# Block inverse of the delta net: from the second level on, even and odd heads on the two 64-row halves of the TensorE array

## What is computed

```python
k_beta = k * beta[..., None]
L = jnp.where(strict, jnp.einsum('bhncd,bhnjd->bhncj', k_beta, k) * decay, 0.0)
uw = lax.linalg.triangular_solve(eye + L, rhs, left_side=True, lower=True, unit_diagonal=True)
```

## Time and profile before

| | |
|---|---|
| median of three runs | 1870.41 us |
| span of the profiled execution, first to last instruction | 1869.1 us |
| the median less that span (the profiled execution's own whole time is not given apart) | 1.3 us |
| TensorE matmul busy, share of the span | 96% |
| VectorE, ScalarE | 49%, 32% |
| mean granted TensorE clock | 0.991 |

### The profile page before, as it was taken

The page is one execution under the profiler, slowest core; times in us unless marked ns, Lnnn a source line. Parts: engine busy times, 40 slices in busy tenths (PEclk is TensorE's granted clock), DMA queues, the critical chain, the costliest instruction groups (busy, mean ns, idle before and its releaser), DMA issues.

```text
span 1869.1 us, 23868 instructions
## 1 busy us (share of the span) xinstructions
PE 1789.6 (96%) x9684; PEld 1276.0 (68%) x9684; DVE 924.8 (49%) x1574; ACT 603.1 (32%) x1089; POOL 42.6 (2%) x61
## 2 busy tenths in 40 slices
PE   7999999999988999999999999999989999999996
PEld 7878888888867787777776767799773333333332
DVE  5354555555575553554447665574663333323234
ACT  6433233323233332233335542573421111111112
POOL 0000000000000000000000000000021000000000
PEclk9999999999999999999999999999999999999999
DMA  7412222222122222212222122210399999999996
GB/s 275 159 68 91 71 99 81 89 79 102 68 102 79 69 88 80 79 68 102 79 79 79 46 91 90 91 46 13 136 354 392 420 421 420 420 421 420 421 420 261
DMA packets 50751, 325.63 MB, mean 174 GB/s; under 512 B 8088, under 2 KB 8264, under 8 KB 14032
## 3 DMA queue, kind: packets, MB, share of 16 engines
q1 hardware_dynamic: 44320, 305.38, 41.7%
q0 software_dynamic: 6032, 17.39, 2.7%
q10 hardware_dynamic: 288, 1.31, 0.2%
HBM read 322.45 MB, written 5.31 MB: 175 GB/s over the span
## 4 chain that ended last, share of the span: by engine, by line
PE 76%; DMA 10%; DVE 7%; ACT 3%; issue 3%; DVEq 0%; ACTq 0%; SPq 0%; POOLq 0%
PE PJ L583 16%; PE PJ L585 15%; PE PJ L584 15%; PE PJ L2596 8%; PE PJ L2610 4%; DMA m_a<-in_w_moe 3%; DMA m_c<-in_w_moe 3%; DMA m_b<-in_w_moe 3%; PE PB L2622 2%; PE PB L2240 2%; PE PB L2201 1%; PE PB L2233 1%; PE PJ L2347 1%; DVE x L1490 1%; DVE w_lo L1288 1%
## 5 line engine op out<-in xcount | busy, mean ns | idle before, releaser
L583 PE MATMUL PJ<-hT_hi,w_hi 128*128 128x512 f32 x832 | 338.8, 407 | 7.5 <-DVE x L1490 6.1
L585 PE MATMUL PJ<-hT_hi,w_lo 128*128 128x512 f32 x832 | 325.4, 391 | 0.0
L1288 DVE TENSOR_TENSOR w_lo<-w_raw,w_hi 128x1024 fp32r<-128x1024 f32 (+1 forms) x224 | 228.2, 1031 | 196.4 <-ACT w_hi L801 195.6
L584 PE MATMUL PJ<-hT_lo,w_hi 128*128 128x512 f32 x832 | 324.7, 390 | 0.0
L801 ACT ACTIVATE w_hi<-w_raw 128x1024 fp32r<-128x1024 f32 (+1 forms) x224 | 196.1, 899 | 26.1 <-PE PJ L585 24.6
L583 PEld LDWEIGHTS PJ<-hT_hi,w_hi 128*128 128x128 f32 x832 | 156.7, 188 | 54.6 <-issue 20.7
L585 PEld LDWEIGHTS PJ<-hT_hi,w_lo 128*128 128x128 f32 x832 | 156.4, 188 | 34.3
L584 PEld LDWEIGHTS PJ<-hT_lo,w_hi 128*128 128x128 f32 x832 | 156.9, 189 | 33.4 <-issue 3.4
L856 ACT ACTIVATE sc<-sc,stats 128x256 f32<-128x256 f32 (+2 forms) x80 | 43.4, 542 | 328.4 <-DVE stats L1371 328.4
L1948 DVE TENSOR_TENSOR x<-x,PB 128x512 f32<-128x512 f32 x128 | 79.4, 681 | 87.6 <-PE PB L2622 87.5
L583 PE MATMUL PJ<-w_hi,hT_hi 128*128 128x256 f32 x384 | 110.3, 287 | 3.0 <-DVE rt L1449 3.0
(11 more groups left out here) (437 smaller groups left out, 2796.7 us busy)
## 6 DMA issues: line engine op xcount, KB each, us to landing
w_raw<-in_w_all SPq DMA_DIRECT2D x92, 1024.0 KB, 4.8
m_b<-in_w_moe SPq DMA_DIRECT2D x86, 1024.0 KB, 26.6
m_a<-in_w_moe SPq DMA_DIRECT2D x66, 1024.0 KB, 26.0
m_c<-in_w_moe SPq DMA_DIRECT2D x20, 1024.0 KB, 27.1
m_d<-in_w_moe SPq DMA_DIRECT2D x10, 1024.0 KB, 27.6
m_e<-in_w_moe SPq DMA_DIRECT2D x10, 1024.0 KB
aux<-scr_c POOLq DMA_DIRECT2D x6, 512.0 KB, 3.9
aux<-in_decay POOLq DMA_DIRECT2D x6, 512.0 KB, 4.1
```

The source lines that it names most:

```text
L583: pe.matmul(dst, lh, rh, start=start, stop=False)
L584: pe.matmul(dst, lh, rl, start=False, stop=False)
L585: return pe.matmul(dst, ll, rh, start=False, stop=stop)
L1288: dve.tensor_tensor(w_lo[:, n % SPLIT, j * w:(j + 1) * w], w_raw[:, n % RAW, j * w:(j + 1) * w], w_hi[:, n % SPLIT, j * w:(j + 1) * w].bit ...
```

## The change

The masks of levels 2 to 6 are written twice, once for each half of the partitions. `u_product` puts heads 0 and 2 on partitions 0 to 63 and heads 1 and 3 on 64 to 127. The mask product then covers 128 rows x 128 columns. `turn` transposes two heads at once (128x128), which puts an even head's rows on 0 to 63 and the odd head's on 64 to 127; it writes columns 256 to 511 of the chunk's bank, and ScalarE copies 128 rows x 256 columns. `level_product` takes rows 0 to 63 for even heads and 64 to 127 for odd ones; even heads of both chunks of a pair go to the first bank of `PJ[c // 2]`, odd heads to the second. So two chunks share two banks, and the waits at these places are for both chunks of the pair (`c | 1`). The last level's transposes are whole ones as before. The diff:

```diff
+        def even_cols(a, l):
+            return a.rearrange("p (a b q two w) -> p a b q two w", a=2, b=2, two=2, w=1 << l)[:, :, :, :, 0, :]
+        def parity_banks(pj, c, l):
+            return pj.rearrange("p (b z a n) -> p b z a n", b=2, z=4, a=2)[:, :, c % 2, :, :].rearrange(
+                "p b a (q w) -> p a b q w", w=1 << l)
...
-                        act.activation(TT[0:rows, c, :], PJ[c // 2][0:rows, (c % 2) * S:(c % 2 + 1) * S],
-                                       ACT.Copy).then_inc(g_T, 1)
+                        bank = PJ[c // 2][:, (c % 2) * S:(c % 2 + 1) * S]
+                        if l < NLVL - 1:
+                            act.activation(TT[:, c, 0:256], bank[:, 256:S], ACT.Copy).then_inc(g_T, 1)
+                        else:
+                            act.activation(TT[:, c, :], bank, ACT.Copy).then_inc(g_T, 1)
...
-                        dve.tensor_tensor(heads64(U[0:rows, c, 0:256]), heads64(PB[c][0:rows, 0:256]), m,
+                        dve.tensor_tensor(heads64(U[:, c, 0:64 * n]), heads64(PB[c][:, 0:64 * n]), m,
                                           ALU.mult).then_inc(g_uc, 1)
...
-                        dve.wait_ge(g_tmm, 4 * (l - 1) + c + 1)
+                        dve.wait_ge(g_tmm, 4 * (l - 1) + (c if l == 1 else c | 1) + 1)
...
+                            dve.tensor_tensor(even_cols(T_[:, c, :], l), even_cols(T_[:, c, :], l),
+                                              parity_banks(PJ[c // 2][:], c, l), ALU.add).then_inc(g_tup, 1)
...
-                            last = pe.matmul(PB[c][0:64, H64[h]], lt_odd(l)[:, c, H64[h]],
+                            last = pe.matmul(PB[c][ROWS[h % 2], H64[h // 2]], lt_odd(l)[:, c, H64[h]],
                                              half(T_[:, c, H4[h]], l, 0), start=True, stop=True)
...
-                    pe.wait_ge(g_T, n + 1)
+                    pe.wait_ge(g_T, n + 1 if l == 1 else 4 * (l - 1) + (c | 1) + 1)
...
+                            o = h % 2 * S + c % 2 * P + h // 2 * 64
+                            last = pe.matmul(PJ[c // 2][:, o:o + 64], TT[ROWS[h % 2], c, H4[h // 2]],
+                                             U[ROWS[h % 2], c, H64[h // 2]], start=True, stop=True)
...
-                    pe.wait_ge(g_tup, 4 * l + c + 1)
                     if l < NLVL - 1:
+                        pe.wait_ge(g_tup, 4 * l + (c if l == 1 else c | 1) + 1)
                         pe.wait_ge(g_col, cols_turn(l, c))
...
-                            last = pe.transpose(pj_(c, h)[0:64, :], U[:, c, 256 + h * 64:256 + (h + 1) * 64], ident)
+                        for i in range(2, 4):
+                            last = pe.transpose(pj_(c, i), U[:, c, H4[i]], ident)
+                    else:
+                        pe.wait_ge(g_tup, 4 * l + (c | 1) + 1)
+                        for h in range(4):
                             last = pe.transpose(pj_(c, h), T_[:, c, H4[h]], ident)
...
-            m = np.concatenate([m.reshape(-1, 2, s, 64)[:, 1].reshape(64, 64), np.zeros((64, 64), bool)])
+            m = np.tile(m.reshape(-1, 2, s, 64)[:, 1].reshape(64, 64), (2, 1))
```

More of the change, by code:

```diff
@@ L1041, in delta_net @@
                                            half(T_[:, c, :], l + 1, 1), ACT.Copy).then_inc(g_col, 1)
-                    rows = 64 if l < NLVL - 1 else P
                     for c in range(4):
                         act.wait_ge(g_tt, 4 * l + c + 1)
-                        act.activation(TT[0:rows, c, :], PJ[c // 2][0:rows, (c % 2) * S:(c % 2 + 1) * S],
-                                       ACT.Copy).then_inc(g_T, 1)
+                        bank = PJ[c // 2][:, (c % 2) * S:(c % 2 + 1) * S]
[3 more added lines that the diff above has]
+                            act.activation(TT[:, c, :], bank, ACT.Copy).then_inc(g_T, 1)
                 def key_sums(c):
@@ L1595, in delta_net @@
                 for l in range(1, NLVL):
-                    rows = P if l == 1 else 64
-                    m = cst[0:rows, C_LVL + l * P:C_LVL + l * P + 64].unsqueeze(1).broadcast_to([rows, 4, 64])
+                    n = 4 if l == 1 else 2
+                    m = cst[:, C_LVL + l * P:C_LVL + l * P + 64].unsqueeze(1).broadcast_to([P, n, 64])
                     for c in range(4):
                         dve.wait_ge(g_umm, 4 * (l - 1) + c + 1)
-                        dve.tensor_tensor(heads64(U[0:rows, c, 0:256]), heads64(PB[c][0:rows, 0:256]), m,
+                        dve.tensor_tensor(heads64(U[:, c, 0:64 * n]), heads64(PB[c][:, 0:64 * n]), m,
                                           ALU.mult).then_inc(g_uc, 1)
@@ L1603, in delta_net @@
                         dve.wait_ge(g_tup, 4 * (l - 1) + c + 1)
-                        dve.wait_ge(g_tmm, 4 * (l - 1) + c + 1)
-                        dve.tensor_tensor(half(T_[:, c, :], l, 0), half(T_[:, c, :], l, 0),
-                                          pj_(c)[:, 0:256].rearrange("p (q w) -> p q w", w=1 << l),
-                                          ALU.add).then_inc(g_tup, 1)
+                        dve.wait_ge(g_tmm, 4 * (l - 1) + (c if l == 1 else c | 1) + 1)
+                        if l == 1:
+                            dve.tensor_tensor(half(T_[:, c, :], l, 0), half(T_[:, c, :], l, 0),
+                                              pj_(c)[:, 0:256].rearrange("p (q w) -> p q w", w=1 << l),
+                                              ALU.add).then_inc(g_tup, 1)
+                        else:
+                            dve.tensor_tensor(even_cols(T_[:, c, :], l), even_cols(T_[:, c, :], l),
+                                              parity_banks(PJ[c // 2][:], c, l), ALU.add).then_inc(g_tup, 1)
                     if 2 <= l < NLVL - 1:
@@ L2323, in delta_net @@
                 H64 = [slice(h * 64, (h + 1) * 64) for h in range(4)]
+                ROWS = H64[0:2]
                 def u_product(l, c):
@@ L2342, in level_product @@
                     n = 4 * (l - 1) + c
-                    rows = P if l == 1 else 64
-                    pe.wait_ge(g_T, n + 1)
+                    pe.wait_ge(g_T, n + 1 if l == 1 else 4 * (l - 1) + (c | 1) + 1)
                     pe.wait_ge(g_uc, n + 1)
                     for h in range(4):
-                        last = pe.matmul(PJ[c // 2][:, (c % 2) * S + h * 64:(c % 2) * S + (h + 1) * 64],
-                                         TT[0:rows, c, H4[h]], U[0:rows, c, H64[h]], start=True, stop=True)
+                        if l == 1:
+                            last = pe.matmul(PJ[c // 2][:, (c % 2) * S + h * 64:(c % 2) * S + (h + 1) * 64],
+                                             TT[:, c, H4[h]], U[:, c, H64[h]], start=True, stop=True)
+                        else:
+                            o = h % 2 * S + c % 2 * P + h // 2 * 64
+                            last = pe.matmul(PJ[c // 2][:, o:o + 64], TT[ROWS[h % 2], c, H4[h // 2]],
+                                             U[ROWS[h % 2], c, H64[h // 2]], start=True, stop=True)
                     last.then_inc(g_tmm, 1)
                 def turn(l, c):
-                    pe.wait_ge(g_tup, 4 * l + c + 1)
                     if l < NLVL - 1:
+                        pe.wait_ge(g_tup, 4 * l + (c if l == 1 else c | 1) + 1)
                         pe.wait_ge(g_col, cols_turn(l, c))
-                    for h in range(4):
-                        if l < NLVL - 1:
-                            last = pe.transpose(pj_(c, h)[0:64, :], U[:, c, 256 + h * 64:256 + (h + 1) * 64], ident)
-                        else:
+                        for i in range(2, 4):
+                            last = pe.transpose(pj_(c, i), U[:, c, H4[i]], ident)
+                    else:
+                        pe.wait_ge(g_tup, 4 * l + (c | 1) + 1)
+                        for h in range(4):
                             last = pe.transpose(pj_(c, h), T_[:, c, H4[h]], ident)
```

## The result

The changed kernel takes 1855.76 us, median of four runs (1853.26 to 1858.03); the kernel before, timed again beside it, 1871.04. The ratio is 0.9913, with 95% between 0.9901 and 0.9925. Predicted were 1854.6, in a range of 1851.5 to 1861.0. The profiled execution has a span of 1853.1 us, 16.0 less than before. One number hides two things that don't belong together: the stretch of the inverse became 17.7 us shorter, more than the 15.8 that were forecast, and the rest of the profiled execution became 1.7 us longer although nothing was changed there.

What follows compares the result with a forecast made beforehand. TensorE alone was taken to bound the inverse, step behind step. Saving 17.4 us at full clock less 1.6 for low clock gives 15.8: span 1869.1 to 1853.3, plus 1.3 is 1854.6 us, range 1851.5 to 1861.

Steps and rivals of the forecast that it cites:

- TensorE's work: Levels 2 to 6: paired u_product 0.93 us instead of 2.01, level_product 1.79 instead of 3.71; turns 0.90 instead of 1.79.
- The change of tiling mode: Turn to u_product: weight columns go from 128 to 64, one more drain per level; without that rule some 0.5 us less.
- The chain: One level, 3 to 5, from level_product to the next: additions, column copy, last turn, u_product; period 4.88 us.
- Level 2 was to take 5.58: Level 2's period, longer because ScalarE does its exponential (1.91 us) and four copies behind level 1's copies.
- The sum at the full clock: Whole inverse, level 1's last turn to L2387: starts at 1269.45 instead of 1287.07 - 0.2, saving 17.4 us.
- The clock: Granted clock in the inverse: today's low stretches vanish, a third of the new one runs low; 17.4 - 1.6 = 15.8 us saved.
- the 4.9 us of slow turns: Three low-clock stretches at levels 2, 4 and 6 of the kernel before; their cost is taken back within the 17.4.
- the third of the new stretch that I put at the low clock: A third of the new inverse at 1.2 GHz, given TensorE's idle gaps of some 0.9 us in 4.88: -1.6 us.
- end of 6.0: Upper end of the clock loss in the new inverse; a level wholly at 1.2 GHz lasts 5.9 us.
- The rival of the low clock throughout: New inverse wholly at the low clock, through idle gaps and half the records: saved 11.4 us, 1859.0; chance 0.11.
- What the stretch loses the whole kernel loses: Behind the inverse nothing is tied to absolute time, so everything, experts included, shifts earlier by the full saving.
- The 1.3 us between span and median: Added to the profiled execution's forecast span of 1853.3 us to give the median forecast of 1854.6.

Runs made afterwards that it cites:

- s_lp: Changed kernel with level_product issuing a chunk pair's four even-head products first, then the four odd-head ones, from level 2 on: 1862.62 us, ratio 0.9942.
- s_all: Changed kernel with the even-head products of all four chunks ahead of the odd-head ones, in u_product and level_product: 1868.98 us, ratio 0.9990.
- s_both: Changed kernel with even-head products of each chunk pair before the odd-head ones, in both level_product and u_product: 1859.82 us, ratio 0.9939.

## Why the prediction came out right

Predicted were 1854.6 us and measured 1855.76. The mechanism is the forecast one; that the number is only 1.2 us off is in part luck, since three terms missed and cancelled (the last three points below).

- **TensorE's work**: right. A pair costs what one cost, for chains of 64-column products too: 0.93 and 1.73 us from first record to last. The orders above show that this needs neighbours on different halves, or at most two products apart. The change of tiling mode that was put down as one more in each level cost nothing extra: that gap is 0.20 us from record to record, as before.
- **The chain**: right. Forecast 4.88, measured 4.89, over the forecast's way (addition, copy, last turns, `u_product`). No step of it missed by more than 0.1 us. Level 2 was to take 5.58 and took 5.33, and the exponential was the cause, as its removal shows.
- **The sum at the full clock**: 17.4 forecast, with the slow turns in it; the stretch lost 47.81 (1287.16 - 1239.35 in the second profile of before, the same in the first) - 30.13 = 17.7.
- **The clock**: the 4.9 us of slow turns went, as counted. The step that failed is the third of the new stretch that I put at the low clock, -1.6 us: it measured 0, in both profiles. (By the prediction's own end of 6.0 for a stretch wholly at the low clock a third is 2.0, not 1.6, and the forecast would have read 1855.0.) I had rested it on the idle gaps; with gaps of 0.9 us in 4.9 the clock stayed at 1.00 inside the stretch, and so it did in eight of the ten variants. It fell there in both profiles of the kernel before and in those of s_lp and s_all. What separates s_lp from s_both, which has both bad orders and kept the clock, I can't tell from these runs; the spread of s_lp's times suggests that it kept it too in some executions. The rival of the low clock throughout, 1859.0, fell. Whether turns alone bring the clock back, the changed kernel can't show, since it has no low stretch in the inverse; in the kernel before the clock was back at 1.00 behind them.
- **"What the stretch loses the whole kernel loses"**: a step whose miss hid the one above. In the profiled execution the inverse and its scan gave 18.1 us up to the addition to `gz`:

```profile
1294.55 0.69 DVE L1661 TENSOR_TENSOR gz<-gz,gk 128x512 f32<-128x512 f32 x1 [2.77 <-ACT gk L1068]
```

and before

```profile
1312.00 1.42 DVE L1646 TENSOR_TENSOR gz<-gz,gk 128x512 f32<-128x512 f32 x2 [2.77 <-ACT gk L1057]
```

These are 17.45 apart, because the changed kernel came to the inverse 0.6 us later; from the addition to the end it took 558.6 us instead of 557.1. The second part has one visible cause, a low stretch in the expert part behind a wait for weights (start, duration, idle before):

```profile
1718.54 1.94 PE L2631 MATMUL PJ<-m_a,mT 128*64 128x512 f32 x8 [0.47 <-DMA m_a<-in_w_moe]
1722.54 3.63 PE L2617 MATMUL PJ<-m_a,xT 128*64 128x512 f32 x8 [2.06 <-DMA m_a<-in_w_moe]
```

It does not go with the change: from the product behind level 6 to the end this execution took 583.3 us, the eleven other profiles of kernels with the change 580.3 to 583.8, and the two of the kernel before 582.2 and 582.7.

- **The 1.3 us between span and median**: too small, and it hid the low-clock term too. In every execution whose span is on record the whole time is 2.1 to 2.3 us longer than the span. The profiled execution of before was thus some 0.9 us slower than the median that it was set against. The forecast span of 1853.3 met 1853.1; the median lay 2.7 above it, not 1.3.

**What stays open.** The unchanged part ahead of the inverse. The medians differ by 15.3 us, 2.4 less than the stretch's 17.7. The ratio's interval, 14.0 to 18.5 us, holds both, but the other kernels say that the difference is real: for each of the twelve timings of kernels with the change (the changed one twice, ten variants), the median lies nearer to that of before than the stretch accounts for, by 0.4 to 3.6 us. The profiles show where. Both of the kernel before reach level 1's `level_product` at 1239.1 and 1239.2, the twelve of kernels with the change at 1239.7 to 1244.0. Up to 540 us the twelve are between 1.3 us ahead of the first profile of before and 1.3 behind it; from there to 600 each loses 1.0 to 3.1 us on it, and the second profile of before loses nothing. All twelve have a low-clock stretch that starts between 550 and 561, and neither profile of before has one; four lose another 1.1 us at 1044 in the same way. No instruction differs there. So part of the gain is given back by the kernels with the change, and not by one unlucky execution; what brings the clock down there is open, and no experiment here was made for it.

## What to carry to other kernels

Products with 64 rows or 64 weight columns on alternate halves of the array cost half, also when they are as short as their weight load; they should alternate in the queue, since in these kernels TensorE found the other half only about two products ahead. Halving the engine that bounds shows the next chain at once (here 3.6 us of TensorE's work in a level, as reckoned, take 4.9), so work out the path of one period with the waits before spending effort on the engine. And look at the clock of such stretches: here it stayed full with dense pairs where single thin products had lost 5 us to it. Last, read the unchanged parts too: they gave back some 2 us of this gain.

## What the runs showed that I had not expected

- Four products in a row on the same rows cost 0.60 us more in 32 records, not 1.7: a look-ahead of about two products, as the starts suggest, hides most of a bad order; eight in a row cost 1.4.
- The granted clock did not fall in a stretch where TensorE idled 2.7 of 27 us, but had a mean of 0.90 where it was never idle and had thin single products.
- Far from the change, from 550 to 561 us on, a low-clock stretch appeared in all twelve profiles of kernels with the change and in neither of the kernel before.
- With transposes and `u_product` alternating in pairs each change of kind cost about 0.15 us, and all of them 0.7 us of a period of 4.34.
